# HGRN2 mixer: diagonal and first level in one set of 64-column products, narrow levels kept in 32-column blocks

## The chip, the cores and the metric

The kernel runs on one core of one Trainium2 chip. The metric is the device time of one execution in microseconds, lower being better. Five engines work at once: TensorE (PE in the rows, its weight loads PEld), VectorE (DVE), ScalarE (ACT), GpSimd (POOL) and SyncE (SP), which issues the weight transfers. PSUM is the memory into which TensorE writes its products, 8 banks of 512 words in each of 128 partitions; all else lies in SBUF.

## What is computed

Four decoder layers, each a token mixer and a convolutional FFN, over 512 tokens of 1024 channels in float32. The change touches the fourth mixer only, HGRN2 with 8 heads of 128 by 128:

```python
q = proj[..., :HGRN_FD] * (DK ** -0.5)
f = lb + (1.0 - lb) * sigmoid(proj[..., HGRN_FD:2 * HGRN_FD])
log_f, kk = log(f), 1.0 - f
def step(state, inp):                       # chunks of tokens
    qc, kc, vc, gc = inp
    cum = cumsum(gc, axis=1)
    decay = exp(where(causal, cum[:, :, None] - cum[:, None, :], -inf))
    attn = einsum('blhk,blshk,bshk->blsh', qc, decay, kc)
    o = einsum('blsh,bshv->blhv', attn, vc) + einsum('blhk,bhkv->blhv', qc * exp(cum), state)
    ...
```

The decay differs in each of the 128 key channels, so that the matrix of query against key is no single product.

## The kernel before

Every weight product is made of two: a rounded float32 part (L295 for the projections in, L337 for those out) and a bf16 remainder (L305, L341). Weight panels of 128 by 1024 words come through a ring of four: SP loads a panel, ACT rounds it (L250), POOL takes the remainder in four pieces (L266), PE uses both. In this mixer a head has four panels (f, q, i, g), and each is used in two halves of four products with L295 and four with L305.

The matrix of a head is built by levels, on keys in rows and queries in columns, four chunks of 128 tokens side by side in `b.attn`. Level 0 is the diagonal (`q` against `ks`). Level n from 1 to 7 has blocks of B = 1, 2, 4, ... 64 tokens (`LEVELS[n - 1]`): the later block of each pair asks, the earlier one answers, with `qp` and `ks`, which carry the decay gathered so far. PE makes a level (`level`, with `narrow` for B up to 16, L1833, and `wide` for 32 and 64, L1848), always with 32 keys at a time as weights, which write the 32 partitions that belong to them. `narrow` has 16 products: of 32 moved columns at level 0 and of 16 at levels 1 to 5. `wide` has 8, of 32 or 64 columns. Then DVE does an update and a copy: L2018, L2019 and L2021 multiply the decays, `qp` and `ks` in place for the next level, and a predicated copy with a mask (L2037 at level 0, L2032 later) puts the products into `b.attn`. PE's next level waits for L2021 by `hgrn_update`, and the copies are counted by `hgrn_attn`, since two PSUM banks (5 and 6) take turns.

`hgrn_events` writes the order out by hand. A head takes eight slots, one for each half panel, `half(h, 0)` to `half(h, 7)`. Level n of head h stands at slot 8h + 5 + n, so that levels 3 to 7 of a head lie under the half panels 0 to 4 of the next. On DVE the level comes first in a slot and the work for the half panel after it (`level_first=True`); on PE it is the other way round. The work for the half panels on DVE is L1983 (f), L1986, L1990 (`ks`), L1991 (`q`), L1995 (`qp` = q times f), L1997 (i) and L2001 (g). The `tail` of a head follows in later slots: transposes L1860 and L1866, products of the state L1871, state on DVE L2045 and L2048, the output L1879 and L1882, the mean of squares L1887, and the normalisation on DVE L2053, L2058, L2061. In the last head no half panels are left, and parts of the output projection (`early`, L337 and L341) stand between its levels.

The level groups wait for these: level 0 for `ks` and `q` (L1991), level 1 for `qp` (L1995), later ones for L2021 of the level before.

## Time and profile before

| | us |
|---|---|
| median of 3 runs | 1772.92 |
| lowest and highest | 1772.85, 1773.04 |
| the profiled execution | 1772.94 |
| its span in the trace | 1771.1 |

The span is from the first instruction to the last; the execution has 1.8 us more around it. PE is busy for 97% of the span, and the granted clock of TensorE is 1.000 over the whole of it. The projections and levels of the fourth mixer lie between 1303 and 1505 us. Rows of a timeline have a start, a duration, the engine, the line, the operation and its tiles, and in brackets the idle time before it with its releaser. A duration is that of an operation through its pipeline, so that the next one of the same engine starts before it is over: what an operation costs in a full queue is the distance between two starts.

### The profile page before, as it was taken

Reading aid. Unit: us, or ns where it says so; the run is one execution under the profiler, and the core shown is the slowest. Engines: PE = TensorE matmul, PEld = TensorE weight load, DVE = VectorE, ACT = ScalarE, POOL = GpSimd, SP = SyncE. Lnnn points to the kernel's source line nnn. Section 1 sums busy time; section 2 is a strip of 40 time slices with the busy share of each in tenths; the row PEclk is TensorE's granted clock in tenths of the full one; section 3 lists DMA queues with packets and bytes.
Section 4 is the critical chain, followed back from the end, with each engine's and each line's share of the span. In section 5 each row is a group of like instructions: output and inputs, shape, how many; then the busy total and the mean of one; then the engine's idle time right before and its main releaser. Section 6 shows DMA issues by size and latency. Waiting matters only on the chain.

```text
span 1771.1 us, 27487 instructions
## 1 busy us (share of the span) xinstructions
PE 1720.5 (97%) x9861; PEld 1040.6 (59%) x10032; DVE 1150.9 (65%) x1873; ACT 1129.3 (64%) x1581; POOL 1227.8 (69%) x1788
## 2 busy tenths in 40 slices
PE   7989999999999999999999999999999999999999
PEld 4546666655555556666665666666655565566665
DVE  6886777228888754777226857776248877577720
ACT  8887666455977757666555877665454555866642
POOL 7747777877555647777877657778865554677785
PEclk9999999999999999999999999999999999999999
DMA  7323444545223225444543114444532222344453
GB/s 270 107 96 120 152 145 148 154 154 158 74 95 104 86 82 175 147 144 149 153 149 108 37 38 150 152 143 147 154 128 97 97 96 73 108 154 145 152 153 122
DMA packets 65615, 226.59 MB, mean 128 GB/s; under 512 B 8149, under 2 KB 9173, under 8 KB 64981
## 3 DMA queue, kind: packets, MB, share of 16 engines
q1 hardware_dynamic: 64236, 221.88, 39.6%
q10 hardware_dynamic: 1245, 2.95, 0.5%
q8 instruction: 80, 1.31, 0.3%
q14 instruction: 54, 0.44, 0.1%
HBM read 222.51 MB, written 2.10 MB: 127 GB/s over the span
## 4 chain that ended last, share of the span: by engine, by line
PE 73%; DVE 10%; ACT 8%; issue 5%; POOL 3%; DMA 1%; ACTq 0%; DVEq 0%; POOLq 0%
PE psum L295 22%; PE psum L305 21%; PE psum L337 12%; PE psum L341 11%; POOL w_rest L266 2%; ACT w_big L250 2%; DMA y_rest<-in_ssd_tables 1%; DVE psum L1621 1%; PE psum L1833 1%; PE psum L2241 1%; ACT psum L1468 1%; PE psum L2276 1%; DVE psum L1706 1%; PE psum L2258 1%; ACT L1501 1%
## 5 line engine op out<-in xcount | busy, mean ns | idle before, releaser
L266 POOL TENSOR_TENSOR w_rest<-w_panel,w_big 128x256 bf16<-128x256 f32 x1660 | 1163.9, 740 | 461.1 <-ACT w_big L250 461.1
L295 PE MATMUL psum<-x_big,w_big 128*128 128x512 f32 x2248 | 656.1, 425 | 8.5 <-ACT x_big L387 6.4
L305 PE MATMUL psum<-x_rest,w_rest 128*128 128x512 bf16 x2131 | 537.7, 382 | 8.7 <-DVE x_rest L483 1.7
L250 ACT ACTIVATE w_big<-w_panel 128x1024 fp32r<-128x1024 f32 (+1 forms) x415 | 418.4, 1032 | 171.9 <-PE psum L341 91.4
L295 PEld LDWEIGHTS psum<-x_big,w_big 128*128 128x128 f32 x2248 | 416.3, 189 | 134.7 <-issue 25.8
L305 PEld LDWEIGHTS psum<-x_rest,w_rest 128*128 128x128 bf16 x2248 | 188.6, 98 | 283.2 <-issue 102.6
L701 DVE SCALAR_TENSOR_TENSOR psum<-ffn_raw,params,psum 128x512 f32<-128x512 f32 x352 | 264.6, 752 | 7.2 <-ACT psum L655 1.0
L693 DVE TENSOR_TENSOR ffn_raw<-psum,rstd 128x512 f32<-128x512 f32 x176 | 121.4, 691 | 138.9 <-PE psum L305 120.3
L655 ACT ACTIVATE psum<-ffn_raw,params 128x512 f32<-128x512 f32 x176 | 137.4, 782 | 102.1 <-DVE ffn_raw L693 101.8
L337 PE MATMUL psum<-g_big,w_big 128*128 128x512 f32 x704 | 199.4, 423 | 0.0
L547 DVE SCALAR_TENSOR_TENSOR x_resid<-psum,x_resid 128x512 f32<-128x512 f32 x64 | 43.8, 689 | 225.0 <-PE psum L341 202.2
L341 PE MATMUL psum<-g_rest,w_rest 128*128 128x512 bf16 x677 | 165.4, 381 | 1.3
L337 PEld LDWEIGHTS psum<-g_big,w_big 128*128 128x128 f32 x704 | 133.2, 189 | 36.0
L662 ACT ACTIVATE g_big<-psum 128x512 fp32r<-128x512 f32 x88 | 52.5, 597 | 111.2 <-DVE psum L710 111.1
L341 PEld LDWEIGHTS psum<-g_rest,w_rest 128*128 128x128 bf16 x704 | 61.1, 98 | 87.8 <-issue 26.5
L337 PE MATMUL psum<-y_big,w_big 128*128 128x512 f32 x320 | 107.8, 459 | 2.1 <-DVE y_rest L2061 1.1
L483 DVE SCALAR_TENSOR_TENSOR x_rest<-x_big,psum 128x512 bf16<-128x512 f32 x64 | 43.9, 686 | 90.7 <-ACT psum L391 90.7
L341 PE MATMUL psum<-y_rest,w_rest 128*128 128x512 bf16 x298 | 84.1, 383 | 2.5 <-POOL w_rest L266 1.8
L337 PEld LDWEIGHTS psum<-y_big,w_big 128*128 128x128 f32 x320 | 60.3, 191 | 18.8 <-issue 5.2
L710 DVE TENSOR_TENSOR psum<-psum,ffn_silu_out 128x512 f32<-128x512 f32 x88 | 61.5, 699 | 7.0 <-ACT ffn_silu_out L678 4.1
L387 ACT ACTIVATE x_big<-x_resid,shifted_gain 128x512 fp32r<-128x512 f32 x64 | 45.4, 710 | 31.6 <-DVE x_resid L547 31.6
L714 DVE SCALAR_TENSOR_TENSOR g_rest<-g_big,psum 128x512 bf16<-128x512 f32 x88 | 59.8, 680 | 2.7 <-ACT g_big L662 2.7
(263 smaller groups left out, 1714.1 us busy)
## 6 DMA issues: line engine op xcount, KB each, us to landing
w_panel<-in_up SPq DMA_DIRECT2D x176, 512.0 KB, 3.5
w_panel<-in_dn SPq DMA_DIRECT2D x64, 448.0 KB, 3.3
w_panel<-in_ssd_in SPq DMA_DIRECT2D x41, 512.0 KB, 3.2
w_panel<-in_dn SPq DMA_DIRECT2D x32, 512.0 KB, 3.5
w_panel<-in_hgrn_in SPq DMA_DIRECT2D x32, 512.0 KB, 3.2
w_panel<-in_lru_in SPq DMA_DIRECT2D x18, 512.0 KB, 3.5
w_panel<-in_ssd_out SPq DMA_DIRECT2D x16, 512.0 KB, 3.2
w_panel<-in_swa_in SPq DMA_DIRECT2D x12, 512.0 KB, 3.2
```

Source lines behind the costliest of these rows:

```text
L250: act.activation(k.w1[:, slot, 0:words], k.w[:, slot, 0:words], ACT.Copy, scale=(SHIFT - 1) / SHIFT).then_inc(k.s("panel_big"), 1)
L266: rest = pool.tensor_tensor(k.w2[:, slot, a], k.w[:, slot, a], k.w1[:, slot, a].bitcast(F32), ALU.subtract)
L295: pe.matmul(out, k.w1[:, slot, q * m:(q + 1) * m], k.x1[:, q, :], start=q == 0, stop=False)
L305: mm = pe.matmul(out, k.w2[:, slot, q * m:(q + 1) * m], k.x2[:, q, :], start=False, stop=q == DT - 1)
L337: pe.matmul(out, k.w1[:, slot, (q - p0) * P:(q - p0 + 1) * P], y1[:, q, :], start=q == 0, stop=False)
L341: mm = pe.matmul(out, k.w2[:, slot, (q - p0) * P:(q - p0 + 1) * P], y2[:, q, :], start=False, stop=q == kt - 1)
L655: act.activation(out, k.ffn_raw[:, j % 2, half, 2:], ACT.Identity, bias=k.p("ffn_conv_b", j + (l * 2 * FF_T + half * FF_T)), scale=k.p("ff ...
L662: act.activation(k.g1[:, j, :], k.ps[:, lin_bank(j), :], ACT.Copy, scale=1 / SHIFT).then_inc(k.s("ffn_hi"), 1)
L693: dve.tensor_tensor(k.ffn_raw[:, j % 2, half, 2:], k.ps[:, k.bank(job, i), :], k.rstd[:, :], ALU.mult).then_inc(k.s("banks_free"), 1)
L701: dve.scalar_tensor_tensor(out, k.ffn_raw[:, j % 2, half, tap:tap + S], k.p("ffn_conv_w", j + ((l * 3 + tap) * 2 * FF_T + half * FF_T)), o ...
L710: dve.tensor_tensor(out, out, k.ffn_silu[:, j % 2, :], ALU.mult).then_inc(k.s("ffn_gated"), 1)
L714: dve.scalar_tensor_tensor(k.g2[:, j, :], k.g1[:, j, :].bitcast(F32), 1 - SHIFT, k.ps[:, lin_bank(j), :], ALU.mult, ALU.add).then_inc(k.s( ...
```

## The change

1. The products of levels 0 and 1 are made by one group, `first_two`: 16 products of 64 moved columns, 32 of `q` and 32 of `qp`, which now lie in one array `queries`. The group stands at the place of level 0 and waits for `hgrn_gates` at 3h + 3, which L1995 gives, where level 0 waited for 3h + 2 (L1991). At the place of level 1 PE has nothing.
2. DVE's update of level 1 waits for this group.
3. The products of levels 1 to 5 lie densely in their bank, 64 words for a partition instead of 256, and the copies of levels 0 to 5 go into `near`, 32 columns for each chunk, in place of the whole matrix. Level 0 copies 128 words in each partition instead of 512, levels 1 to 5 copy 64 instead of 256.
4. After the copy of level 5 four plain copies of 32 partitions by 4 by 32 words put `near` on the diagonal of `b.attn`. Levels 6 and 7 copy as before.
5. A mask more, and a memset of `near` (128 words) before the first head. The banks are counted by `level_bank`, the copies of a head by `HG_COPIES` = 12.

```diff
 HG_BLOCK = 32
+HG_NEAR = 5
+HG_COPIES = len(LEVELS) + 1 + P // HG_BLOCK
 HG_LATE = (0, 1, 2, 3, 4, 5, 7, 8, 9)
...
         a = Arena(k)
-        self.q, self.ks, self.qp = a.take(2, S), a.take(2, S), a.take(2, S)
+        self.queries, self.ks = a.take(2, 2, S), a.take(2, S)
+        self.q, self.qp = self.queries[:, 0], self.queries[:, 1]
         self.f = a.take(S)
...
-        self.masks = a.take(len(LEVELS), P // 2, dt=I32)
+        self.masks = a.take(len(LEVELS) + 1, P // 2, dt=I32)
+        self.near = a.take(NC, HG_BLOCK)
...
+def level_bank(k, h, n):
+
+    return k.ps[:, 5 + (len(LEVELS) * h + max(n, 1) - 1) % 2, :]
+
...
     def level(h, n):
         if n == 0:
-            pe.wait_ge(k.s("hgrn_gates"), 3 * h + 2)
+            pe.wait_ge(k.s("hgrn_gates"), 3 * h + 3)
             pe.wait_ge(k.s("banks_free"), k.evicted(job, 4 * h + 1))
-        elif n == 1:
-            pe.wait_ge(k.s("hgrn_gates"), 3 * h + 3)
-        else:
+            if h:
+                pe.wait_ge(k.s("hgrn_attn"), HG_COPIES * h - 1)
+            first_two(h).then_inc(k.s("hgrn_level"), 1)
+        elif n > 1:
             pe.wait_ge(k.s("hgrn_update"), 21 * h + 3 * (n - 1))
-        done = 8 * h + n
-        if done >= 2:
-            pe.wait_ge(k.s("hgrn_attn"), done - 1)
-        (wide if n and LEVELS[n - 1] >= HG_BLOCK else narrow)(h, n).then_inc(k.s("hgrn_level"), 1)
-
-    def narrow(h, n):
+            if h or n > 2:
+                pe.wait_ge(k.s("hgrn_attn"), HG_COPIES * h + (n - 1 if n > 2 else 0))
+            (wide if n > HG_NEAR else narrow)(h, n).then_inc(k.s("hgrn_level"), 1)
+
+    def first_two(h):

         for c in range(NC):
             for first in range(0, P, HG_BLOCK):
                 keys = slice(c * P + first, c * P + first + HG_BLOCK)
-                if n:
-                    at, size = c * P // 2 + first // 2, HG_BLOCK // 2
-                    rhs = in_halves(b.qp[:, h % 2, keys], LEVELS[n - 1])[:, :, 1, :]
-                else:
-                    at, size, rhs = c * P + first, HG_BLOCK, b.q[:, h % 2, keys]
-                mm = pe.matmul(k.ps[first:first + HG_BLOCK, 5 + n % 2, at:at + size], b.ks[:, h % 2, keys], rhs,
-                               start=True, stop=True)
+                out = level_bank(k, h, 0)[first:first + HG_BLOCK, 2 * c * HG_BLOCK:2 * (c + 1) * HG_BLOCK]
+                mm = pe.matmul(out.rearrange("p (two l) -> p two l", two=2), b.ks[:, h % 2, keys],
+                               b.queries[:, :, h % 2, keys], start=True, stop=True)
+        return mm
+
+    def narrow(h, n):
+
+        near = level_bank(k, h, n)[:, 0:NC * HG_BLOCK // 2].rearrange("p (c l) -> p c l", c=NC)
+        for c in range(NC):
+            for first in range(0, P, HG_BLOCK):
+                keys = slice(c * P + first, c * P + first + HG_BLOCK)
+                rhs = in_halves(b.qp[:, h % 2, keys], LEVELS[n - 1])[:, :, 1, :]
+                mm = pe.matmul(near[first:first + HG_BLOCK, c], b.ks[:, h % 2, keys], rhs, start=True, stop=True)
         return mm
...
         elif t == 3:
             pe.wait_ge(k.s("hgrn_state"), 3 * (h + 1))
-            pe.wait_ge(k.s("hgrn_attn"), 8 * (h + 1))
+            pe.wait_ge(k.s("hgrn_attn"), HG_COPIES * (h + 1))
...
     chain(dve.memset(b.attn, 0.0))
+    chain(dve.memset(b.near, 0.0))
     dve.wait_ge(k.s("mixer_landed"), 128)
...
-            dve.wait_ge(k.s("hgrn_level"), 8 * h + n + 1)
+            dve.wait_ge(k.s("hgrn_level"), 7 * h + n)
...
                               ).then_inc(k.s("hgrn_update"), 1)
-            dve.wait_ge(k.s("hgrn_attn"), 8 * h + n)
         else:
-            dve.wait_ge(k.s("hgrn_lb"), 12)
-            dve.wait_ge(k.s("hgrn_level"), 8 * h + 1)
+            dve.wait_ge(k.s("hgrn_lb"), 13)
+            dve.wait_ge(k.s("hgrn_level"), 7 * h + 1)
+        done = HG_COPIES * h + n + (P // HG_BLOCK if n > HG_NEAR else 0)
+        if done:
+            dve.wait_ge(k.s("hgrn_attn"), done)
         attn = b.attn[:, h % 2, :].rearrange("p (c l) -> p c l", c=NC)
-        if n:
-            attn = attn.rearrange("p c (n two b) -> p c n two b", two=2, b=B)[:, :, :, 1, :]
-            ps = k.ps[:, 5 + n % 2, 0:S // 2].rearrange("p (c n b) -> p c n b", c=NC, b=B)
-            mask = b.masks[:, n - 1, :].rearrange("p (n b) -> p n b", b=B).unsqueeze(1)
-            dve.copy_predicated(attn, mask.to_broadcast([P, NC, P // 2 // B, B]), ps
-                                ).then_inc(k.s("hgrn_attn"), 1)
+        ps = level_bank(k, h, n)
+        both = ps[:, 0:2 * NC * HG_BLOCK].rearrange("p (c two l) -> p c two l", c=NC, two=2)
+        if n == 0:
+            ident = b.masks[:, len(LEVELS), 0:HG_BLOCK].unsqueeze(1).to_broadcast([P, NC, HG_BLOCK])
+            dve.copy_predicated(b.near, ident, both[:, :, 0, :]).then_inc(k.s("hgrn_attn"), 1)
+            return
+        span_, to = (P, attn) if n > HG_NEAR else (HG_BLOCK, b.near)
+        to = to.rearrange("p c (n two b) -> p c n two b", two=2, b=B)[:, :, :, 1, :]
+        if n == 1:
+            ps = both[:, :, 1, :].rearrange("p c (n two b) -> p c n two b", two=2, b=1)[:, :, :, 1, :]
+        elif n > HG_NEAR:
+            ps = ps[:, 0:S // 2].rearrange("p (c n b) -> p c n b", c=NC, b=B)
         else:
-            ps = k.ps[:, 5, :].rearrange("p (c l) -> p c l", c=NC)
-            ident = k.c("ident").bitcast(I32).unsqueeze(1).to_broadcast([P, NC, P])
-            dve.copy_predicated(attn, ident, ps).then_inc(k.s("hgrn_attn"), 1)
+            ps = ps[:, 0:NC * HG_BLOCK // 2].rearrange("p (c n b) -> p c n b", c=NC, b=B)
+        mask = b.masks[:, n - 1, 0:span_ // 2].rearrange("p (n b) -> p n b", b=B).unsqueeze(1)
+        dve.copy_predicated(to, mask.to_broadcast([P, NC, span_ // 2 // B, B]), ps).then_inc(k.s("hgrn_attn"), 1)
+        if n == HG_NEAR:
+            dve.wait_ge(k.s("hgrn_attn"), done + 1)
+            for first in range(0, P, HG_BLOCK):
+                own = slice(first, first + HG_BLOCK)
+                dve.tensor_copy(attn[own, :, own], b.near[own]).then_inc(k.s("hgrn_attn"), 1)
...
     s, n = np.arange(P)[:, None], np.arange(P // 2)[None]
-    m = [(s // (2 * B) == n // B) & (s // B % 2 == 0) for B in LEVELS]
+    near = s % HG_BLOCK
+    m = [((s if B >= HG_BLOCK else near) // (2 * B) == n // B) & (s // B % 2 == 0) for B in LEVELS] + [near == n]
     return np.stack(m, axis=1).astype(np.int32)
```

How the order moves on PE, at levels 0 and 1 of the third head (`narrow` L1833 and `first_two` L1838; L1860 and L1875 are the same transposes, as are L1866 and L1881). Before:

```order
L1833 MATMUL psum<-arena 32x32 [waits hgrn_attn,banks_free,hgrn_gates]
L1833 MATMUL psum<-arena 32x32 x15
L1860 MATMUL psum<-consts,arena 128x128 [waits hgrn_rstd_log,banks_free]
L1860 MATMUL psum<-consts,arena 128x128 x3
L295 MATMUL psum<-x_big,w_big 128x512 [waits banks_free,panel_big]
L295 MATMUL psum<-x_big,w_big 128x512 x3
L305 MATMUL psum<-x_rest,w_rest 128x512 [waits panel_split]
L305 MATMUL psum<-x_rest,w_rest 128x512 x3
L1833 MATMUL psum<-arena 32x16 [waits hgrn_attn,hgrn_gates]
L1833 MATMUL psum<-arena 32x16 x15
L1866 MATMUL psum<-consts,arena 128x128 [waits hgrn_update,hgrn_i_t]
L1866 MATMUL psum<-consts,arena 128x128 x2
```

and now:

```order
L1838 MATMUL psum<-arena 32x64 [waits hgrn_attn,banks_free,hgrn_gates]
L1838 MATMUL psum<-arena 32x64 x15
L1875 MATMUL psum<-consts,arena 128x128 [waits hgrn_rstd_log,banks_free]
L1875 MATMUL psum<-consts,arena 128x128 x3
L295 MATMUL psum<-x_big,w_big 128x512 [waits banks_free,panel_big]
L295 MATMUL psum<-x_big,w_big 128x512 x3
L305 MATMUL psum<-x_rest,w_rest 128x512 [waits panel_split]
L305 MATMUL psum<-x_rest,w_rest 128x512 x3
L1881 MATMUL psum<-consts,arena 128x128 [waits hgrn_update,hgrn_i_t]
L1881 MATMUL psum<-consts,arena 128x128 x2
```

One group of 16 is gone, and the transposes L1881 follow the half panel directly.

On DVE, at level 5 of the second head, which lies between the f projection of the next head (L1983 before, L1999 now) and L1986 (now L2002). Before:

```order
L1983 TENSOR_TENSOR arena<-psum,rstd 128x512 [waits hgrn_update,panel_used]
L2018 TENSOR_TENSOR arena<-arena 128x16 [waits hgrn_update,hgrn_level]
L2019 TENSOR_TENSOR arena<-arena 128x16x16
L2021 TENSOR_TENSOR arena<-arena 128x16x16
L2032 COPY_PREDICATED arena<-arena,psum 128x16x16 [waits hgrn_attn]
L1986 TENSOR_SCALAR arena<-arena 128x512 [waits hgrn_tanh]
L2018 TENSOR_TENSOR arena<-arena 128x8 [waits hgrn_update,hgrn_level]
```

and now:

```order
L1999 TENSOR_TENSOR arena<-psum,rstd 128x512 [waits hgrn_update,panel_used]
L2034 TENSOR_TENSOR arena<-arena 128x16 [waits hgrn_update,hgrn_level]
L2035 TENSOR_TENSOR arena<-arena 128x16x16
L2037 TENSOR_TENSOR arena<-arena 128x16x16
L2061 COPY_PREDICATED arena<-arena,psum 128x4x16 [waits hgrn_attn]
L2066 COPY arena<-arena 32x4x32 [waits hgrn_attn]
L2066 COPY arena<-arena 32x4x32 x3
L2002 TENSOR_SCALAR arena<-arena 128x512 [waits hgrn_tanh]
L2034 TENSOR_TENSOR arena<-arena 128x8 [waits hgrn_update,hgrn_level]
```

The copy is a quarter as large, and four copies stand between it and the next head's work and level 6.

## Rows read from the trace of the kernel before

**Rows 1.** The page, part 1: busy time, share and count of each engine.
```profile
PE 1720.5 (97%) x9861; PEld 1040.6 (59%) x10032; DVE 1150.9 (65%) x1873; ACT 1129.3 (64%) x1581; POOL 1227.8 (69%) x1788
```
**Rows 2.** Timeline of PE, levels 6 and 7 of the third head, then the fourth.
```profile
1379.86 0.45 PE L1848 MATMUL psum<-arena 128*32 128x32 f32 x16
...
1382.24 0.64 PE L1848 MATMUL psum<-arena 128*32 128x64 f32 x16
1382.81 1.21 PE L295 MATMUL psum<-x_big,w_big 128*128 128x512 f32 x4
...
1384.83 0.46 PE L1833 MATMUL psum<-arena 128*32 128x32 f32 x32
1385.22 0.66 PE L1860 MATMUL psum<-consts,arena 128*128 128x128 f32 x4
...
1387.61 0.45 PE L1833 MATMUL psum<-arena 128*32 128x16 f32 x32
1387.98 0.55 PE L1866 MATMUL psum<-consts,arena 128*128 128x128 f32 x3
...
1393.31 0.45 PE L1833 MATMUL psum<-arena 128*32 128x16 f32 x32
1393.92 0.71 PE L1879 MATMUL psum<-arena 128*128 128x128 f32 x4 [0.16 <-DVE arena L2048]
```
**Rows 3.** Timeline of DVE in the same stretch.
```profile
1380.35 0.38 DVE L2018 TENSOR_TENSOR arena<-arena 128x8 f32<-128x8 f32 x1 [0.52 <-PE psum L1848]
...
1380.99 0.95 DVE L2021 TENSOR_TENSOR arena<-arena 128x256 f32<-128x256 f32 x1
1381.87 0.43 DVE L2032 COPY_PREDICATED arena<-arena,psum 128x256 f32<-128x256 int32 x1
...
1384.41 0.68 DVE L1995 TENSOR_TENSOR arena<-arena 128x512 f32<-128x512 f32 x1
...
1390.78 0.29 DVE L2018 TENSOR_TENSOR arena<-arena 128x128 f32<-128x128 f32 x1 [0.40 <-PE psum L1833]
1390.99 0.42 DVE L2019 TENSOR_TENSOR arena<-arena 128x256 f32<-128x256 f32 x1
```
**Rows 4.** Timeline of the first head and the start of the second, PE.
```profile
1317.67 0.46 PE L1833 MATMUL psum<-arena 128*32 128x32 f32 x32 [0.89 <-DVE arena L1991]
...
1322.86 0.45 PE L1833 MATMUL psum<-arena 128*32 128x16 f32 x32 [0.35 <-DVE arena L2021]
...
1338.32 0.46 PE L1833 MATMUL psum<-arena 128*32 128x32 f32 x32
```
**Rows 5.** The same, DVE.
```profile
1316.49 0.43 DVE L1990 TENSOR_SCALAR arena<-arena 128x512 f32<-128x512 f32 x1
1316.83 0.69 DVE L1991 SCALAR_TENSOR_TENSOR arena<-psum,rstd 128x512 f32<-128x512 f32 x1
1317.55 1.24 DVE L1995 TENSOR_TENSOR arena<-arena 128x512 f32<-128x512 f32 x1
...
1328.16 0.50 DVE L2018 TENSOR_TENSOR arena<-arena 128x32 f32<-128x32 f32 x1 [1.14 <-PE psum L1833]
1328.59 1.01 DVE L2019 TENSOR_TENSOR arena<-arena 128x256 f32<-128x256 f32 x1
...
1339.27 0.89 DVE L1995 TENSOR_TENSOR arena<-arena 128x512 f32<-128x512 f32 x1
```
**Rows 6.** Chain of waits, third head: start us, us on the chain, products of L295.
```profile
1380.30 1.12 PE psum L295 x4
...
1385.88 0.92 PE psum L295 x4
```
**Rows 7.** Timeline of the last head, DVE and PE, levels 6 and 7.
```profile
1494.80 0.17 DVE L2018 TENSOR_TENSOR arena<-arena 128x8 f32<-128x8 f32 x1 [0.19 <-PE psum L1848]
...
1495.22 0.42 DVE L2021 TENSOR_TENSOR arena<-arena 128x256 f32<-128x256 f32 x1
...
1495.80 0.64 PE L1848 MATMUL psum<-arena 128*32 128x64 f32 x16
```

2 lines of the change are left out of this document (1 added, 1 removed).

## The prediction

> **What bounds the kernel now.** The page comes first: TensorE is busy for 97% of the span, DVE for 65% [rows 1], so what PE issues less of is time, unless PE then waits for something else. The timeline of PE over one cycle of levels [rows 2] shows the groups of levels standing between half panels, with a new one every 2.4 to 3.1 us and nearly no idle time: the only wait in brackets there is 0.16 us at L1879, the output product, for DVE's L2048. It comes back in the later heads. The timeline of DVE in the same stretch [rows 3] is the second view, since the change also moves a wait: it puts TensorE's first group of a head behind L1995. There the reader should look at where DVE stands idle (0.52 us before L2018 of level 6, until PE's group is done) and at where it doesn't: from 1380.35 to the end of L1995 DVE works without a gap. The start of the mixer is different [rows 4, 5]: DVE is behind, PE waits for it, and L1995 takes 1.24 and 0.89 us in place of 0.68.
>
> **The products of a head.** Group against group, by the distance of starts: level 0 took 1385.22 - 1384.83 = 0.39 us, level 1 took 1387.98 - 1387.61 = 0.37 us [rows 2]. The second is removed: -0.37. The first gets 64 columns instead of 32, which the trace doesn't show for 16 products. The bound below is 0.39 us, that columns cost nothing. For the bound above, level 7 has 8 products of 64 columns in 1382.81 - 1382.24 = 0.57 us, 71 ns each, so that 16 would take 1.14 us. But level 7 writes only two of the four 32-partition strips, and level 0 all four. Level 6, also on two strips, has 8 products of 32 columns in a row 0.19 us shorter (0.45 against 0.64), so 0.38 us or 48 ns each, and level 0 pays half of that, 24 ns, with four strips. The same half for 64 columns is 36 ns, and 16 of them 0.57 us. I take that: +0.18 against level 0. Beside it, TensorEngine Tiling ("Instruction Overhead") of the Trainium skill says that a product with few moved columns costs the same as one of about 60. Rows 2 agree for 16 against 32 columns (0.37 and 0.39 us); by the rule alone the first group would stay near 0.39 us, and the sum below would be 8 x 0.18 = 1.4 us less.
>
> **The wait that it adds.** L1995 ends at 1384.41 + 0.68 = 1385.09 [rows 3], while PE began level 0 at 1384.83 [rows 2]. PE passes work to DVE in 0.04 us (level 6 ends at 1380.31, L2018 starts at 1380.35); with 0.06 us for the other direction the new group starts at 1385.15, 0.32 us late: +0.32 a head. PE takes instructions in order, so the transposes L1860 and the next half panel stand behind this wait, and ScalarE behind the transposes; DVE loses nothing, as its next step that needs the group is the copy of level 0. L1995 can't come earlier by a faster level 0 to 5, since the stretch before it begins with PE's own group of level 6, 1385.09 - 1379.86 = 5.23 us before its end.
>
> **The wait that it takes away.** DVE's update of level 1 no longer waits for a group of its own, and the copies of levels 0 to 2 are smaller, so that L2048 comes over half a microsecond earlier against PE's level 3. L1879 started at 1393.92, and could have at 1393.31 + 0.37 = 1393.68 [rows 2]: -0.24. After that nothing is late before the next head's L1995.
>
> **The copies.** The copy of a level from 3 to 7 is a row of 0.43 us [rows 3]. The pipeline hides 0.08 of a row (L2018 lasts 0.29 and its successor starts 0.21 later), so it costs 0.35; with 0.06 of it fixed and a quarter of the words the new one costs 0.13, a saving of about 0.20 each. It is under work that PE doesn't wait for, except where DVE is behind. Against it stand four plain copies of 128 words a partition and one wait for the copy of level 5 (0.08, one pipeline). No such copy is in the trace. By the fastest row between SBUF tiles, L1990 with 512 words in 1316.83 - 1316.49 = 0.34 us [rows 5], it could be 0.085; by the row of the same size, L2018 with 128 words, 0.21 [rows 3]; next to a busy POOL even a row of 32 words took 1328.59 - 1328.16 = 0.43 us [rows 5]. L1990 has one tile as source and is the nearest in kind: 0.06 fixed and 0.55 ns a word give 0.13. I take 0.15 for the unknown layout: 4 x 0.15 + 0.08 = 0.68 us a head. They stand before the update of level 6, which had 0.52 us of idle time before it, and the copy of level 5 gives 0.20 back. So 0.68 just fits into 0.72, and costs nothing in the middle heads. Were the cover gone, each further 0.1 us would move L1995, and with it PE's first group, by 0.1 us in every head.
>
> **A middle head** is then -0.37 + 0.18 + 0.32 - 0.24 = -0.11 us, and from the first group of the second head to that of the last there are six: -0.66.
>
> **The first head.** The memset of `near` adds some 0.2 us (128 words, as L2018) ahead of it. L1995 ends at 1317.55 + 1.24 = 1318.79 [rows 5], the group can start at 1319.05, and it started at 1317.67 [rows 4]: +1.38. Back come 0.37 for level 1, less 0.18 for the columns; 0.20 because four products of L295 cost 1.12 on the chain right behind a level group and 0.92 elsewhere [rows 6], and this head has no transposes in between; and the 0.35 that PE waited for L2021 at level 2 [rows 4]. That leaves +0.64 at level 2. From level 4 on (1328.16, [rows 5]) DVE has no idle time until the second head's L1995 ends at 1339.27 + 0.89 = 1340.16, and PE's level groups wait for it. In that stretch 2 x 0.20 are saved and 0.68 added: +0.28. L1995 ends at 1341.08, the group starts at 1341.14 instead of 1338.32 [rows 4]: **+2.82**.
>
> **The last head.** Level 2 comes 0.37 - 0.18 = 0.19 earlier against the first group, the copy of level 2 brings L2048, for which PE waits, forward by at least 0.20. Then 0.68 - 0.20 stand against 0.19 of idle time before level 6 and the 0.10 by which L2021 (end 1495.64, plus 0.06) preceded PE's level 7 at 1495.80 [rows 7]: +0.19. Together -0.20. What follows (normalisation, output projection, FFN) is a chain from here and shifts as a whole. The mask and its transfer are loaded long before and cost nothing.
>
> **Sum.** 2.82 - 0.66 - 0.20 = +1.96 us on the profiled execution of 1772.94, which is at the median of the runs (1772.92): **1774.9 us**. The products win 0.19 x 8 = 1.5 us, and it goes to L1995, most of it in the first head. With both lower bounds (no cost of columns, 0.085 a copy) the sum is 1.96 - 1.44 - 0.5 = 0, 1773.0.
>
> **Rivals.** 1. *The copies make DVE the bound, and it is slower.* Place: the four L2066 copies before the update of level 6. The point is 0.16 us each; for it speaks that POOL's pieces stretch DVE's rows between SBUF tiles (L2021 of 0.95 against L2019 of 0.42 [rows 3]), against it that POOL rests at this place in the middle heads. At 0.21 us (+0.24 a head) the first head gives 3.06, six heads (0.20 - 0.11) x 6 = 0.54, the last +0.04: 1776.6. At 0.28 us it is 3.34 + 2.2 + 0.3: 1778.8; at 0.43 near 1784. Its time is 1778.5. The Trainium skill, Advanced Engine Details and Errata ("VectorE Performance Modes"), lets a copy between SBUF tiles run at double rate over a port shared with GpSimd, so that each blocks the other; the row of 0.95 agrees with the blocking.
>
> 2. *The wait for L1995 isn't there, and the products count.* If the update of level 6 met no POOL piece, L2021 would be 0.42 and L2018 about 0.16, 0.75 us less ahead of L1995, and the 0.32 were gone. Six heads give -0.43 x 6 = -2.58, the first +2.5, the last -0.20: -0.3 or 1772.6; with columns at no cost too, 1771.2. Against it: POOL starts by ScalarE's rounding of a panel, which keeps its place against the half panels.
>
> 3. *The 64 columns don't overlap over the strips as 32 do*, since `q` and `qp` are read from two places: 1.14 us a group, 8 x 0.57 = 4.6 more, 1779.5. The four strips of level 0 speak against it. This is also the case in which the merged group doesn't do what it should, one pass for two.
>
> **Chances.** My forecast with its bounds, 1773.0 to 1777.5: 0.52. Copies: 0.20. No wait: 0.20. Strips: 0.05. The rest 0.03. 0.2% of 1772.92 is 3.5 us, about what a measurement of this kernel tells from no change, so that faster means below 1769.4 (the end of the second rival, 0.07) and slower above 1776.5 (the first and third rival, and the upper end of the forecast: 0.28). The rest, 0.65, is no change. The range leaves out the dearest copies and strips and the cheapest of the second rival: 1771.0 to 1779.0.
>
> **What would show it.** In the trace of the changed kernel: L1838 groups of 0.57 us by distance of starts; in each middle head an idle time of some 0.3 us before L1838, released by L2011 (the former L1995); no wait at L1894 (the former L1879) for L2077; L2066 at 0.13 to 0.17 us from start to start, with the idle time before the update of level 6 nearly gone; the second head's first group near 1341.1 and from then on a cycle 0.1 us shorter than before. The forecast falls if L1838 has no wait, if L2066 is above 0.16 us apart, or if DVE in the first head is relieved by POOL taking other turns, in which case the 2.82 is too high.

## The result and the profile after

| | before | changed |
|---|---|---|
| median, us | 1772.93 (4 runs) | 1790.07 (4 runs) |
| lowest and highest | 1772.85, 1773.04 | 1787.75, 1791.44 |
| ratio with 95% interval | | 1.0096, 1.0084 to 1.0108 |
| span of the profiled execution | 1771.1 | 1785.9 |

The change makes the kernel 17 us slower. The forecast was 1774.9 us with a range of 1771.0 to 1779.0, so the time lies far outside. The profiled execution has the lowest of the four times, 1787.75 us; its span is 14.8 us longer than before, and it is this difference that the two traces can account for.

The other 2.3 us go with TensorE's clock. The profiled execution has a granted clock of 1.000, as every execution of the kernel before has. The other three of the changed kernel have a mean of 0.997 to 0.999 and take 2.0 to 3.7 us more. Their traces aren't kept, but eight of the runs below show what such a mean can be: one or two stretches of 3.4 us at half clock (1.2 GHz instead of 2.4), which begin between 0.1 us before and 1.3 us after PE takes up its work again behind a wait of 1.8 to 3.0 us in the first two heads. In the run without copies the stretch lies behind the second head's wait; four products of L295, which take 1.2 us elsewhere, take 2.06:

```profile
1340.79 0.65 PE L1838 MATMUL psum<-arena 128*32 128x64 f32 x32 [1.80 <-DVE arena L2011]
1341.97 2.06 PE L295 MATMUL psum<-x_big,w_big 128*128 128x512 f32 x4
```

In the view of this stretch by windows the third number from the end is the granted clock, 0.50:

```profile
1341.60:1345.00 3.40, 3.15 (x10) 1.99 (x10) 2.06 (x6) 0.60 (x1) 0.00 (x0) 0.50 0.36 136
```

This head's cycle, from its first group to that of the next head, lasts 24.89 us, the later ones 23.27. So one such stretch costs 1.6 us. The forecast and the expectations of the runs have nothing on this.

The waits of PE over the whole span, changed kernel (total us, times, longest us). Before there is none for L1995, and 0.7 us in two waits for L2021 at levels 6 and 7 (L1848):

```profile
PE psum L1838 <- DVE arena L2011: 12.0, 8, 2.3
PE psum L1863 <- DVE arena L2037: 8.4, 9, 3.0
```

L2011 is the former L1995, L2037 the former L2021, L1863 the former L1848. So PE waits for DVE at two places of a middle head. The wait at L1879 of [rows 2] is gone there: L1894 starts without one. The timeline of PE, changed kernel, levels 6 and 7 of the third head and the first groups of the fourth, which answers to [rows 2]:

```profile
1385.13 0.45 PE L1863 MATMUL psum<-arena 128*32 128x32 f32 x16
...
1388.32 0.64 PE L1863 MATMUL psum<-arena 128*32 128x64 f32 x16 [0.74 <-DVE arena L2037]
...
1392.49 0.65 PE L1838 MATMUL psum<-arena 128*32 128x64 f32 x32 [1.53 <-DVE arena L2011]
1393.08 0.66 PE L1875 MATMUL psum<-consts,arena 128*128 128x128 f32 x4
...
1400.66 0.45 PE L1849 MATMUL psum<-arena 128*32 128x16 f32 x32
1401.03 0.71 PE L1894 MATMUL psum<-arena 128*128 128x128 f32 x4
```

and DVE and POOL beside it, the view of [rows 3]:

```profile
1384.01 0.22 DVE L2061 COPY_PREDICATED arena<-arena,psum 128x64 f32<-128x64 int32 x1
1384.27 2.37 DVE L2066 COPY arena<-arena 32x128 f32<-32x128 f32 x4
1386.67 0.85 DVE L2002 TENSOR_SCALAR arena<-arena 128x512 f32<-128x512 f32 x1
...
1391.56 0.88 DVE L2011 TENSOR_TENSOR arena<-arena 128x512 f32<-128x512 f32 x1
```

```profile
1384.45 2.79 POOL L266 TENSOR_TENSOR w_rest<-w_panel,w_big 128x256 bf16<-128x256 f32 x4 [1.84 <-ACT w_big L250]
1389.34 3.69 POOL L266 TENSOR_TENSOR w_rest<-w_panel,w_big 128x256 bf16<-128x256 f32 x4 [2.10 <-ACT w_big L250]
```

The four copies take 2.37 us: the first, which starts ahead of POOL, 0.21, the others 0.74, 0.66 and 0.67. POOL's four pieces begin 0.18 us after the first copy and keep their 0.70 us each. From there DVE works without a gap until L2011 ends at 1392.44, and is late both to level 7 (PE waits 0.74 us) and to the merged group (1.53 us). The last head of the changed kernel has no POOL piece at this place, and there the same four copies take 0.97 us, in the timeline of DVE:

```profile
1508.68 0.97 DVE L2066 COPY arena<-arena 32x128 f32<-32x128 f32 x4
```

Where the 14.8 us come from, by the starts of the first level group of a head (level 0 before, the merged group now) in the two timelines:

| first group of | before | changed | behind | forecast |
|---|---|---|---|---|
| head 1 | 1317.67 | 1318.87 | 1.20 | 1.38 |
| head 2 | 1338.32 | 1342.30 | 3.98 | 2.82 |
| head 4 | 1384.83 | 1392.49 | 7.66 | 2.60 |
| head 8 | 1477.88 | 1492.86 | 14.98 | 2.16 |
| end of the span | 1771.1 | 1785.9 | 14.8 | 1.96 |

A middle head takes (1492.86 - 1342.30) / 6 = 25.09 us instead of (1477.88 - 1338.32) / 6 = 23.26: +1.83 where -0.11 was forecast, 11.0 us over six. From the last head's first group to the end 0.2 us come back, as forecast.

### The profile page after: what moved, and what is told of

It reads as the page before. It is cut to its first block, busy times and chain, and to the rows that moved or that the text cites. A ratio compares the mean times of both kernels' runs of the same rounds, so it can differ in the third digit from the quotient of the medians.

```text
span 1785.9 us, 27000 instructions
## 1 busy us (share of the span) xinstructions
PE 1718.0 (96%) x9605; PEld 1039.0 (58%) x9776; DVE 1156.5 (65%) x1906; ACT 1129.2 (63%) x1581; POOL 1230.2 (69%) x1788
## 3 DMA queue, kind: packets, MB, share of 16 engines
q8 instruction: 78, 1.28, 0.3%
## 4 chain that ended last, share of the span: by engine, by line
PE 71%; DVE 12%; ACT 8%; issue 5%; POOL 2%; DMA 1%; ACTq 0%; SPq 0%; DVEq 0%; POOLq 0%
PE psum L295 21%; PE psum L305 20%; PE psum L337 12%; PE psum L341 11%; POOL w_rest L266 2%; ACT w_big L250 1%; DMA y_rest<-in_ssd_tables 1%; DVE psum L1621 1%; DVE arena L2066 1%; DVE arena L2037 1%; PE psum L2270 1%; ACT psum L1468 1%; PE psum L1849 1%; PE psum L2305 1%; DVE psum L1706 1%
## 5 line engine op out<-in xcount | busy, mean ns | idle before, releaser
L295 PE MATMUL psum<-x_big,w_big 128*128 128x512 f32 x2248 | 656.0, 425 | 8.6 <-ACT x_big L387 6.5
L305 PE MATMUL psum<-x_rest,w_rest 128*128 128x512 bf16 x2131 | 537.7, 381 | 8.7 <-DVE x_rest L483 1.7
L250 ACT ACTIVATE w_big<-w_panel 128x1024 fp32r<-128x1024 f32 (+1 forms) x415 | 418.4, 1032 | 171.9 <-PE psum L341 91.4
L295 PEld LDWEIGHTS psum<-x_big,w_big 128*128 128x128 f32 x2248 | 416.1, 189 | 135.2 <-issue 25.9
L305 PEld LDWEIGHTS psum<-x_rest,w_rest 128*128 128x128 bf16 x2248 | 188.6, 98 | 283.2 <-issue 102.1
```

The lines of the kernel that those rows point to most:

```text
L250: act.activation(k.w1[:, slot, 0:words], k.w[:, slot, 0:words], ACT.Copy, scale=(SHIFT - 1) / SHIFT).then_inc(k.s("panel_big"), 1)
L295: pe.matmul(out, k.w1[:, slot, q * m:(q + 1) * m], k.x1[:, q, :], start=q == 0, stop=False)
L305: mm = pe.matmul(out, k.w2[:, slot, q * m:(q + 1) * m], k.x2[:, q, :], start=False, stop=q == DT - 1)
```

## Experiments

Theory A: the four copies are dear because copies between two SBUF tiles take turns with POOL's pieces, DVE comes late, and the merged group, which now waits for DVE's last step for the head, pays a second time. Theory B: the merged group's later start is the loss by itself. Each ratio is against the kernel before on the same chip in the same session, where its medians were 1772.8 to 1773.0 us. The changes shown leave out the counts and waits that merely go with them, where "..." or the text says so.

### The four copies left out

The diagonal blocks then never reach the matrix. `HG_COPIES` is four less, and the count of the next copy goes with it.

```diff
-        if n == HG_NEAR:
-            dve.wait_ge(k.s("hgrn_attn"), done + 1)
-            for first in range(0, P, HG_BLOCK):
-                own = slice(first, first + HG_BLOCK)
-                dve.tensor_copy(attn[own, :, own], b.near[own]).then_inc(k.s("hgrn_attn"), 1)
```

> The changed kernel without its four plain copies (L2066) a head, so that the diagonal blocks never reach the matrix and this part is left out of the result. Theory A, the four copies are the loss: they took 2.37 us a head against 0.68 in my sum and made DVE late for level 7 and L2011. Without them the sum goes as forecast less 0.68 in the first and last head and nothing in the others: about 1774 us, a cycle of 23.1 us a head, waits of PE of 0.3 us a head for L2011 and none for L2037 at level 7. Theory B, the later start of the merged group (it waits for q times f) is the loss: PE still waits some 1.5 us a head for L2011, 1785 us or more.

Measured: 1776.7 us, ratio 1.0024 (1.0014 to 1.0033). Of the 17 us 13 are gone with the copies. What stays, 3.7 us, is more than forecast. The timeline of PE and of DVE without copies, fourth head:

```profile
1385.78 0.64 PE L1863 MATMUL psum<-arena 128*32 128x64 f32 x16
1388.95 0.65 PE L1838 MATMUL psum<-arena 128*32 128x64 f32 x32 [0.51 <-DVE arena L2011]
...
1412.22 0.65 PE L1838 MATMUL psum<-arena 128*32 128x64 f32 x32 [0.51 <-DVE arena L2011]
```

```profile
1387.95 0.95 DVE L2011 TENSOR_TENSOR arena<-arena 128x512 f32<-128x512 f32 x1
```

A cycle takes 1412.22 - 1388.95 = 23.27 us, as before: all that the merged group and the gone wait at L1894 (the former L1879) win is spent on L2011. From level 7 to the first group it is 3.17 us against 2.59 before, a wait of 0.58 by distance and not 0.32, since L2011 takes 0.95 us instead of 0.68.

The 3.7 us themselves lie ahead of the third head. The merged group of the second head starts at 1340.79, 2.5 us later than before, behind a wait of 1.80 us for L2011, and that of the third at 1365.68, 4.1 us later, 1.6 us of it the half clock shown above; 0.7 us come back in the last head. All ten executions have a granted clock of 0.998 or 0.999.

### The copies read PSUM

They take the bank of level 5, so PE's level 7, which writes this bank next, has to wait for them too; they are over at 1385.78, 2.4 us before the end of L2037, for which it waits.

```diff
-                pe.wait_ge(k.s("hgrn_attn"), HG_COPIES * h + (n - 1 if n > 2 else 0))
+                pe.wait_ge(k.s("hgrn_attn"), HG_COPIES * h + (10 if n == 7 else n - 1 if n > 2 else 0))
...
+            raw_ps = level_bank(k, h, n)[:, 0:NC * HG_BLOCK].rearrange("p (c l) -> p c l", c=NC)
...
-                dve.tensor_copy(attn[own, :, own], b.near[own]).then_inc(k.s("hgrn_attn"), 1)
+                dve.tensor_copy(attn[own, :, own], raw_ps[own]).then_inc(k.s("hgrn_attn"), 1)
```

> The four copies read the PSUM bank of level 5 instead of the block store in SBUF: same count, same words, same target; the content of the diagonal blocks is left out. Theory A1, a copy between two SBUF tiles takes turns with POOL's pieces (one copy for each piece of 0.70 us), and one that reads PSUM doesn't: the four take 0.9 to 1.1 us in every head, POOL's pieces beside them stay at 0.70 us, 1776 to 1777 us. Theory A2, a copy of 32 partitions into a strided target is slow by itself: they still take 2.4 us, 1790 us.

Measured: 1784.5 us, 1.0064 (1.0049 to 1.0079), between both expectations. The rows side with A1: the four copies, beside a POOL that works on its pieces as before, last 1.24 us and each one 0.28 us, at most 0.30.

```profile
1384.54 1.24 DVE L2067 COPY arena<-psum 32x128 f32<-32x128 f32 x4
...
1384.69 3.23 POOL L266 TENSOR_TENSOR w_rest<-w_panel,w_big 128x256 bf16<-128x256 f32 x4 [1.83 <-ACT w_big L250]
```

Target layout and number of partitions are the same, so they are not what makes 2.37 us. But copies that POOL doesn't stretch still cost 7.8 us against the run without them. They aren't small: 0.31 us each from start to start, and they push DVE's level 6 update into the pieces of POOL (its L2034 then takes 0.70 us and L2037 0.94). PE still waits 0.44 us at level 7 and 1.15 for L2011. So my expectation of 1776 us counted the copies alone and not what they are pushed into.

### POOL quiet, changed kernel and kernel before

POOL makes one piece of 2 words for each of the 32 panels of this mixer's projections in, and the bf16 remainder of these panels is left out. The panels of the projection out keep their pieces.

```diff
-    for at in range(0, words, PIECE):
-        a = slice(at, min(at + PIECE, words))
+    for at in (0,) if PANELS[n][0] == "hgrn_in" else range(0, words, PIECE):
+        a = slice(at, at + 2) if PANELS[n][0] == "hgrn_in" else slice(at, min(at + PIECE, words))
```

> The changed kernel with POOL's four pieces of a panel cut to one of 2 words for the 32 projection panels of this mixer; the bf16 remainder of these panels is left out. Theory A1: the four copies take about 1.0 us in every head, as they did in the last head, and L2037 and L2002 lose their long rows too: 1771 to 1775 us. Theory A2: still 2.4 us and 1790 us.

> The kernel before with the same pieces of POOL left out, as the base for the run before this one. PE bounds the middle heads, so only the waits of the first head go: 1771 to 1772.5 us. Theory A1 puts the changed kernel within 2 us of this one; theory A2 puts it 17 us above.

Measured: the changed kernel 1771.6 us (0.9993, 0.9984 to 1.0003), the kernel before 1771.5 us (0.9991, 0.9982 to 1.0000). The kernel before hardly notices that POOL is quiet; the changed one loses its whole disadvantage, 18 us. The timeline of DVE, POOL quiet, changed kernel:

```profile
1376.94 0.97 DVE L2066 COPY arena<-arena 32x128 f32<-32x128 f32 x4
1377.94 0.55 DVE L2002 TENSOR_SCALAR arena<-arena 128x512 f32<-128x512 f32 x1
```

and of PE, whose last two lines are level 7 of the seventh head and the merged group of the last:

```profile
1380.15 0.64 PE L1863 MATMUL psum<-arena 128*32 128x64 f32 x16
1382.75 0.65 PE L1838 MATMUL psum<-arena 128*32 128x64 f32 x32
...
1405.44 0.65 PE L1838 MATMUL psum<-arena 128*32 128x64 f32 x32
...
1471.87 0.64 PE L1863 MATMUL psum<-arena 128*32 128x64 f32 x16 [0.75 <-DVE arena L2037]
...
1476.10 0.65 PE L1838 MATMUL psum<-arena 128*32 128x64 f32 x32 [1.59 <-DVE arena L2011]
```

The four copies take 0.97 us as in the last head above. The cycle is 22.69 us against 23.26 of the kernel before with POOL quiet: this is what the change wins where nothing stands in its way, 0.57 us a head. It comes in five cycles and is used up at both ends. In the first head PE waits 1.80 us for L2011. And in the last cycle, 25.28 us, POOL works again, on panels of the projection out from 1466.73 on; the copies there take 1.70 us, and both waits of the changed kernel are back.

### One of the two parts alone

Levels 0 and 1 as two groups again in the changed kernel, with the banks and counts of the kernel before; store and copies kept:

```diff
-            pe.wait_ge(k.s("hgrn_gates"), 3 * h + 3)
+            pe.wait_ge(k.s("hgrn_gates"), 3 * h + 2)
...
-            first_two(h).then_inc(k.s("hgrn_level"), 1)
-        elif n > 1:
+        elif n == 1:
+            pe.wait_ge(k.s("hgrn_gates"), 3 * h + 3)
+        else:
```

> The changed kernel with levels 0 and 1 as two groups again, 16 products of 32 and 16 of 16 moved columns, with the waits of the kernel before; block store and four copies stay. The copies still meet POOL and take 2.4 us, so PE waits 0.7 us a head at level 7, but no longer for L2011. Theory A (the copies make DVE late, and the merged group then waits for the late L2011): a cycle of 23.25 + 0.74 - 0.24 = 23.75 us, some 3 us for the six middle heads and 3 us in the first, 1779 us. Theory A' (the copies are the loss wherever the group stands): as the changed kernel, 1788 us or more. Theory B (the merged group alone is the loss): back to 1773 us.

Measured: 1780.6 us, 1.0045 (1.0030 to 1.0060). The copies are there and PE waits at level 7 as in the changed kernel, but nothing waits for L2011:

```profile
1387.13 0.64 PE L1863 MATMUL psum<-arena 128*32 128x64 f32 x16 [0.75 <-DVE arena L2037]
1389.71 0.46 PE L1849 MATMUL psum<-arena 128*32 128x32 f32 x32
```

The other way round, the kernel before with the wait alone:

```diff
-            pe.wait_ge(k.s("hgrn_gates"), 3 * h + 2)
+            pe.wait_ge(k.s("hgrn_gates"), 3 * h + 3)
```

> The kernel before with one number changed: level 0 waits for L1995 (q times f) instead of L1991. By my sum this wait is 0.32 us in each middle head, 1.2 us in the first and up to 1.9 us at the start of the second, where DVE is behind: 1775 to 1778 us. Theory B wants 8 us or more here, 1781 us.

Measured: 1780.9 us, 1.0047 (1.0032 to 1.0062). One number in one wait costs 8 us; I had expected 2 to 5, and this is the time that theory B asked for. The profiled execution is the slowest of the four, 1783.0 us. In it the third head's first group comes at 1367.99, 6.4 us later than before, behind waits of 2.08 and 1.79 us, each followed by a stretch of 3.4 us at half clock; the second head's cycle lasts 25.60 us, the later ones 23.97. The middle heads have 0.7 us each. The timelines of PE, DVE and POOL:

```profile
1388.68 0.64 PE L1848 MATMUL psum<-arena 128*32 128x64 f32 x16
1392.00 0.46 PE L1833 MATMUL psum<-arena 128*32 128x32 f32 x32 [0.66 <-DVE arena L1995]
```

```profile
1391.05 0.89 DVE L1995 TENSOR_TENSOR arena<-arena 128x512 f32<-128x512 f32 x1
```

```profile
1390.66 3.27 POOL L266 TENSOR_TENSOR w_rest<-w_panel,w_big 128x256 bf16<-128x256 f32 x4 [1.49 <-ACT w_big L250]
```

Level 7 to level 0 is 3.32 us against 2.59, a wait of 0.73. Before, POOL's pieces began at 1384.87, after L1995 had started at 1384.41 [rows 3]; here they begin 0.39 us ahead of it, and it lasts 0.89 us instead of 0.68. In both traces POOL begins these pieces 7.25 us after the f projection on DVE (at 1377.62 before, at 1383.40 here), but L1995 comes 6.79 us after it before and 7.65 here. So holding PE back moves POOL against DVE, and that doubles the wait I had worked out from a timeline in which PE wasn't held.

Last, four copies added to the kernel before, between scratch tiles:

```diff
+            if n == 5:
...
+                for first in range(0, P, HG_BLOCK):
+                    own = slice(first, first + HG_BLOCK)
+                    dve.tensor_copy(b.far[own, :, own], b.near[own]).then_inc(k.s("hgrn_lb"), 1)
```

> The kernel before with four copies of 32 partitions by 4 by 32 words added after the copy of level 5, between two scratch tiles in SBUF with the same strides; nothing reads them. Everything else of the kernel before. Theory A: the copies take 1.2 to 2.4 us a head (POOL's pieces start about 1 us after them here), L2021 of level 6 is late for level 7 by 0.4 to 1.2 us a head, and level 0 has slack: 1777 to 1783 us. Theory B: no more than 1 us above the kernel before.

Measured: 1785.4 us, 1.0069 (1.0052 to 1.0086), 2.4 us above the expected range. PE waits at level 7 in every head, 10.6 us in all, and the heads take turns between two patterns. The third head and the fourth, DVE, POOL and PE:

```profile
1385.16 1.40 DVE L2042 COPY arena<-arena 32x128 f32<-32x128 f32 x4
1385.71 3.27 POOL L266 TENSOR_TENSOR w_rest<-w_panel,w_big 128x256 bf16<-128x256 f32 x4 [2.90 <-ACT w_big L250]
1389.31 0.64 PE L1849 MATMUL psum<-arena 128*32 128x64 f32 x16 [1.27 <-DVE arena L2023]
...
1409.53 2.30 DVE L2042 COPY arena<-arena 32x128 f32<-32x128 f32 x4
1409.63 2.81 POOL L266 TENSOR_TENSOR w_rest<-w_panel,w_big 128x256 bf16<-128x256 f32 x4 [2.04 <-ACT w_big L250]
1413.51 0.64 PE L1849 MATMUL psum<-arena 128*32 128x64 f32 x16 [0.90 <-DVE arena L2023]
```

In the third POOL starts as late as in the kernel before, the first three copies take 0.22 us each and only the fourth 0.65, and all four take 1.40 us. Yet PE waits longer, 1.27 us, because L2020 and L2023 of the level 6 update now stand among POOL's pieces (0.68 and 0.94 us). In the fourth the copies take 2.30 us and the update behind them is short again.

Against the kernel before: the wait alone +8, the copies alone +12.4, the merged group without copies +3.7, all together +17. Neither theory holds alone. B is refuted as the whole by the run without copies, 1776.7 us where it wanted 1785 or more, but its wait is dear wherever the products' gain doesn't pay for it.

### What a copy's price depends on

One copy of 128 partitions instead of four of 32; three of the four diagonal blocks are left out (counts not shown):

```diff
-            for first in range(0, P, HG_BLOCK):
-                own = slice(first, first + HG_BLOCK)
-                dve.tensor_copy(attn[own, :, own], b.near[own]).then_inc(k.s("hgrn_attn"), 1)
+            dve.tensor_copy(attn[:, :, 0:HG_BLOCK], b.near).then_inc(k.s("hgrn_attn"), 1)
```

> The changed kernel with one copy of all 128 partitions by 4 by 32 words into one column block in place of four copies of 32 partitions into their own; the diagonal blocks of three of four strips are left out. Same words for a partition, one instruction. Theory A1 (each copy that meets POOL waits for one of its pieces of 0.70 us): at most 0.7 us a head, and about 0.3 if it is through before POOL starts, so close to the run without copies, 1776.5 to 1779 us. If the price goes by words moved or by the target's layout it is far less than a quarter cheaper: 1785 us or more.

Measured: 1777.1 us, 1.0020 (1.0011 to 1.0030), the time without copies. The one copy is all but through when POOL starts, so this run doesn't show what a copy of 128 partitions costs beside it:

```profile
1383.27 0.23 DVE L2064 COPY arena<-arena 128x128 f32<-128x128 f32 x1
1383.43 3.42 POOL L266 TENSOR_TENSOR w_rest<-w_panel,w_big 128x256 bf16<-128x256 f32 x4 [1.84 <-ACT w_big L250]
```

Four copies with a quarter of the words each; three of four chunks of the diagonal blocks are left out:

```diff
-                dve.tensor_copy(attn[own, :, own], b.near[own]).then_inc(k.s("hgrn_attn"), 1)
+                dve.tensor_copy(attn[own, 0:1, own], b.near[own, 0:1]).then_inc(k.s("hgrn_attn"), 1)
```

> The changed kernel with the same four copies of a quarter of the words each (one chunk of the four; the other three chunks of the diagonal blocks are left out). Theory A1, a turn with POOL for each copy whatever its size: still 1.7 to 2.4 us for the four in the middle heads, 1786 to 1790 us. If words count: four copies of 32 words take some 0.5 us, 1777 to 1779 us.

Measured: 1789.9 us, 1.0095 (1.0080 to 1.0110), the time of the changed kernel.

```profile
1385.93 2.32 DVE L2066 COPY arena<-arena 32x32 f32<-32x32 f32 x4
```

A quarter of the words saves 0.05 us of 2.37. Beside a working POOL each of these copies between SBUF tiles costs its turn, about one piece of 0.70 us, with 128 words as with 32, and the number of instructions is what counts.

### Versions without the loss

The copies on ScalarE, after it has evicted the transposed state keys, two stores in turn (`near[:, h % 2]`), the group where the change has it (the waits of PE and DVE for these copies aren't shown):

```diff
+            act.wait_ge(k.s("hgrn_attn"), HG_COPIES * (h + 1))
+            attn = b.attn[:, h % 2, :].rearrange("p (c l) -> p c l", c=NC)
+            for first in range(0, P, HG_BLOCK):
+                own = slice(first, first + HG_BLOCK)
+                act.activation(attn[own, :, own], b.near[own, h % 2], ACT.Copy).then_inc(k.s("hgrn_lb_exp"), 1)
```

> The changed kernel with the four copies on ScalarE and the merged group left where the change has it. Whole result. Theory A: as the run without copies, 1776.7 us, with 0.5 us of waiting for L2011 in the middle heads and a cycle of 23.27 us; the difference to the version of 1769.0 us is then what the place of the group costs. If ScalarE's copies cost something in their new place, above 1778 us.

Measured: 1777.0 us, 1.0023 (1.0013 to 1.0032), the same as with no copies at all: on ScalarE, at this place, they are free.

The same, and q times f ahead of level 7's update on DVE:

```diff
-        ev += levels + halves if level_first else halves + levels
+        ev += levels + halves if level_first and slot % HG_HALVES != 4 else halves + levels
```

> As the run before this one, and on DVE q times f (L2011's place) is computed ahead of the update of level 7 instead of behind its copy. The group stays at level 0's place. Whole result. If the wait for L2011 is what is left of the loss, it ends in the middle heads: a cycle of 22.7 us, and with the first head's two waits still partly there 1770.5 to 1773 us. If level 7's copy or update, now later, holds PE elsewhere, 1775 us or more.

Measured: 1771.6 us, 0.9992 (0.9983 to 1.0001). Only the first head's wait for q times f is left (2.5 us), and the cycle is 22.69 us. Nine executions with a granted clock of 0.999 took 1771.4 to 1771.9 us and the tenth, with 1.000, 1769.9, so that half clock behind this wait costs 1.7 us here.

Copies on ScalarE, and the merged group and the copy of level 0 one slot later, at the place of level 1:

```diff
     def level(h, n):
+        if n:
+            group(h, 0 if n == 1 else n)
+
+    def group(h, n):
         if n == 0:
...
     def level(h, n):
+        if n == 1:
+            place(h, 0)
+        if n:
+            place(h, n)
+
+    def place(h, n):
```

> A version meant to keep the products and drop both costs: the four copies go to ScalarE behind L1925's successor (the state keys), with two block stores in turn, and the merged group and the copy of level 0 stand one slot later, at the place of level 1, where L2011 is long done. Whole result. By theory A nothing of the loss is left: a cycle of 23.25 - 0.37 + 0.20 - 0.24 = 22.84 us or less (22.69 was seen with POOL quiet), that is 2.5 to 3.5 us for the middle heads and about 0 for the first: 1769.5 to 1771.5 us. If DVE's update of level 1, which now stands between the group and level 2 in one slot, comes late, the cycle stays near 23.2 us and the time at 1773 us.

Measured: **1769.0 us, 0.9977 (0.9967 to 0.9986)**, faster than both kernels. The timeline of PE and ScalarE:

```profile
1386.40 0.65 PE L1842 MATMUL psum<-arena 128*32 128x64 f32 x32
...
1409.10 0.65 PE L1842 MATMUL psum<-arena 128*32 128x64 f32 x32
```

```profile
1387.95 1.28 ACT L1951 ACTIVATE arena<-arena 32x128 f32<-32x128 f32 x4
...
1391.51 0.63 ACT L1935 ACTIVATE arena<-arena 128x512 f32<-128x512 f32 x1 [0.97 <-DVE arena L2027]
```

In the middle heads the group starts without a wait. The four copies take 1.28 us on an engine that has room: the tanh behind them still waits 0.97 us for DVE. POOL has no piece beside them in any head of this run or of the one with the group left in place, so how copies on ScalarE fare beside GpSimd isn't shown. The cycle is 22.71 us. The first head is nearly free, since PE does a half panel while DVE makes q times f: its group waits 0.67 us, and the group of the second head, now at the place of level 1, starts at 1340.98, where the kernel before had level 1 at 1341.10. All ten executions have a granted clock of 1.000. Of the 8.0 us between this version and the one with the group left in place 3.4 are six cycles of 0.57 us less; the rest lies at the start, in its waits and the clock behind them, and wasn't taken apart.

Not tried: the four copies on DVE at a place where POOL rests.

## Why the prediction was wrong

**The products were right.** The merged group takes 1393.08 - 1392.49 = 0.59 us against 0.57 forecast, so that the price of 64 columns over four strips came out of the rows of levels 0, 6 and 7. The rule of the Trainium skill that I set beside it (TensorEngine Tiling (Array Packing), "Instruction Overhead"), that a product costs the same up to about 60 columns, would have put it near 0.39 us; here 64 columns cost 0.20 more than 32, and the measurement decides. The strips' rival fell with it. The wait at L1894 vanished as forecast, and the last head came out at -0.2 us. The half panel behind the transposes L1881 even starts 0.16 us earlier than the 0.37 of the missing group explain (1395.62 - 1394.50 = 1.12 us behind L305 where it was 1388.29 - 1386.64 = 1.65): with POOL quiet the cycle is 0.57 us shorter, where my terms give 0.37 - 0.18 + 0.24 = 0.43. That is the case of the second rival, an update of level 6 that meets no piece of POOL: no wait for L2011 in those heads, as it said.

**The step that failed is the price of the copies**, the sentences "I take 0.15 for the unknown layout: 4 x 0.15 + 0.08 = 0.68 us" and "0.68 just fits into 0.72, and costs nothing in the middle heads". They measured 2.37 us. Put into the forecast's own sum, 2.37 + 0.08 where POOL works and 0.97 + 0.08 in the last head, they give +4.59 for the first head, 6 x 1.62 for the middle and +0.17 for the last, 14.5 us, where the trace has 3.98, 11.0 and -0.2, 14.8. So the path was right, DVE's stretch from level 5 to L1995 that ends at PE's first group, and the price of one term on it was wrong. That the two sums agree to 0.3 us is partly luck: the first head came out 0.6 below and the middle ones 0.2 above each.

Two errors lie in the price. First, even without POOL a copy took 0.25 us from start to start (0.97 us for four), not 0.15: the overlap of 0.08 us that I took from neighbouring rows doesn't show between these. With the wait ahead of them it is 1.25 us from L2061 to L2002 (1376.69 to 1377.94), and the slack of 0.72 was gone in any case; the run from PSUM, with 0.31 us each, shows what that costs beside a working POOL, +7.8 us. Second, the turns with POOL. I had the upper bound, 0.43 us for a row beside a busy POOL [rows 5], and gave the rival that used it 0.20 and a price of 1778.5 us, because "POOL rests at this place in the middle heads". It rested until 1.01 us after the start of level 5's copy, long enough for 0.68 us of copies but not for what they take. Before, in the third head into the fourth:

```profile
1377.48 0.45 PE L1833 MATMUL psum<-arena 128*32 128x16 f32 x32
1377.62 0.68 DVE L1983 TENSOR_TENSOR arena<-psum,rstd 128x512 f32<-128x512 f32 x1
...
1378.97 0.43 DVE L2032 COPY_PREDICATED arena<-arena,psum 128x256 f32<-128x256 int32 x1
```

with POOL beside it, where the second row is the run of pieces beside L1995:

```profile
1379.98 3.42 POOL L266 TENSOR_TENSOR w_rest<-w_panel,w_big 128x256 bf16<-128x256 f32 x4 [2.90 <-ACT w_big L250]
1384.87 2.89 POOL L266 TENSOR_TENSOR w_rest<-w_panel,w_big 128x256 bf16<-128x256 f32 x4 [1.47 <-ACT w_big L250]
```

and the same place of the changed kernel:

```profile
1382.08 0.68 DVE L1999 TENSOR_TENSOR arena<-psum,rstd 128x512 f32<-128x512 f32 x1
1382.73 0.45 PE L1849 MATMUL psum<-arena 128*32 128x16 f32 x32
```

The f projection on DVE came 0.14 us after PE's level 5 and now comes 0.65 us ahead of it. ScalarE's tanh hangs on it, behind that the rounding of a panel (L250), behind that POOL's pieces, 2.36 us after the projection before and 2.37 in the changed kernel. The copies hang on PE's level 5 instead. So POOL started 1.01 us after the start of level 5's COPY_PREDICATED before (1379.98 against 1378.97), and starts 0.44 us after it now (1384.45 against 1384.01).

The smaller level copies aren't the whole reason. The update of level 4 meets one piece of POOL less (its first row takes 0.21 us where it took 0.80), and the copy of level 4 is 0.20 us shorter. But the kernel before with the wait alone, whose level copies are as long as ever, has the shorter update too (0.19 us), its f projection 0.52 us ahead of level 5 and POOL 0.57 us behind the copy. Nor is the shift what makes the loss. In the kernel before with copies added, every second head keeps POOL at its old place, and there PE waits more (1.27 us) than in the heads where POOL has moved (0.90). The copies fill the time that DVE had ahead of POOL's pieces; whether they or the update of level 6 then stand among the pieces changes little.

**The wait for L2011** was the second, smaller miss, and it is the case on which the forecast's mechanism was right and its size was off: 0.32 us in the sum, 0.58 without copies and 0.73 in the kernel before with that wait alone. The shifted pieces of POOL stand beside L2011, which takes 0.88 to 0.95 us instead of 0.68. The two waits of the changed kernel, 0.74 us at level 7 and 1.53 at the merged group, are no double payment: DVE has no gap between the copies and the end of L2011, so a PE that hadn't waited at level 7 would have waited that much longer at the merged group. Theory A, as I wrote it above, is wrong in this point. With two groups only the deadline at level 7 is left, a cycle of 23.82 us instead of 25.10.

**The first head** was forecast at +2.82 and came to +3.98: the copies there took 2.60 us and PE waited 3.02 us at level 7; what of DVE's stretch gave the 0.6 us back that the sum with the measured copies has too much wasn't looked into. **The rival that happened** is the first, copies that make DVE the bound, with its place and mechanism, but it is priced at 1778.5 where 0.6 us a copy was needed; at 0.43 I had written "near 1784". The rule cited there from Advanced Engine Details and Errata of the Trainium skill ("VectorE Performance Modes"), that copies between SBUF tiles and GpSimd block each other, describes what the runs show: 2.37 us between SBUF tiles beside POOL, 1.24 from PSUM, 0.97 with POOL quiet. It stood in the text as a remark, and should have decided the price; the row of 0.95 us that I set beside it is a product of two SBUF tiles and not a copy.

## What to carry to other kernels

Small copies between SBUF tiles on DVE are to be counted in instructions, not in words, and each one that may come to stand beside GpSimd at a turn of it, unless an idle engine can take them. Idle time of another engine counts as room only up to its next start, and a new step that fills it pushes the old steps into what follows. A timeline of the kernel before shows where GpSimd works there; a moved wait or a shorter step can shift that. Where a group waits for an engine's last result, try it one place later in its own queue: here that was 8 us. And where TensorE comes to wait some microseconds, look at the granted clock of each execution before comparing times to a microsecond or two.

## What the runs showed of the hardware

- Four copies of 32 partitions between SBUF tiles take 2.37 us beside GpSimd's pieces of 0.70 us and 0.97 us without them; with a quarter of the words still 2.32 us. A copy that starts ahead of the pieces takes 0.21 us, the ones among them 0.66 to 0.74.
- The same copies from PSUM take 1.24 us beside GpSimd, 0.31 us from start to start.
- Copies of 32 partitions between SBUF tiles didn't overlap: 0.25 us from start to start at 0.215 us each.
- On ScalarE, with GpSimd idle, four such copies take 1.28 us.
- 16 products of 64 moved columns over four strips of 32 weight columns take 0.59 us, of 32 columns 0.39, of 16 columns 0.37.
- Behind a wait of TensorE of 1.8 to 3.0 us in the first two heads its granted clock was half for 3.4 us in many executions and in some not, at a price of 1.6 to 1.7 us. In the kernel before, and in the fastest version, where the waits at the level groups of these heads are at most 0.9 us, no execution shows it.
